# Twelve w_mod pieces moved from VectorE to TensorE strips in a two-block transformer kernel

## The chip, the cores and the metric

The kernel runs on one core of a Trainium2 chip. The metric is the time of one execution in microseconds on the device. The kernel before has a median of 2662.97 us over three runs, 2662.01 to 2665.58.

## The reference, cut to what matters

Two transformer blocks run over 256 tokens of width 2048, in float32. The change touches only the first block, and in it one of the six rows that a small vector `c` gives (`scale_m`):

```python
cond = jax.nn.silu(c)
mod = (cond @ w_mod[layer] + b_mod[layer]).astype(x.dtype)          # 2048 x 12288
shift_a, scale_a, gate_a, shift_m, scale_m, gate_m = [
    m[:, None, :] for m in jnp.split(mod, N_MOD, axis=-1)]
h = _rmsnorm(x, pre_mix_g[layer]) * (1.0 + scale_a) + shift_a
proj = h @ w_in[layer]
attn_out = _mla(...)                  # latent attention
rec_out = _hgrn2_bidir(...)           # gated recurrence, forwards and backwards
mix = jnp.concatenate([attn_out, rec_out], axis=-1) @ w_out[layer]
x = x + gate_a * _rmsnorm(mix, post_mix_g[layer])
h = _rmsnorm(x, pre_mlp_g[layer]) * (1.0 + scale_m) + shift_m
```

`w_mod` is 2048 x 12288, so one of the six rows needs 2048 x 2048 floats, 16 MB.

## The kernel before, in words

Every matrix product goes in chunks of 512 KB of weights. SyncE issues a chunk's DMA into one of 4 slots (`w_raw`), ScalarE rounds it (`w_hi`, L1267 or L1270), VectorE subtracts the rounded part (`w_lo`, `remainder`, L1742), and TensorE multiplies with both parts (L780 and L783 where the weights are stationary, L800 to L802 where the tokens are). A slot's DMA waits until VectorE has made `w_lo` of the chunk four before, ScalarE's rounding waits until TensorE has used that chunk (`chunk_used`), and TensorE waits for `w_lo`. So each engine may run up to four chunks ahead of the next one.

Each engine has one order of work, written out by hand. A list of phases (L363 on) says which chunks come; a function `beside` of each engine is called behind each chunk, and says what else that engine does there. The phases around the change are `in_f` (48 chunks), `in_hg` (16 chunks), `w_oa` (16), `w_or` (16), and then `up_0`.

The rows of `w_mod` come in **pieces** of 128 x 1024 floats (512 KB): piece (r, i) has rows 128 r to 128 r + 127 and half i of the columns, so a row of `mod` has 32 pieces. A list beside each phase gives each piece a chunk number. SyncE issues the piece's DMA behind that chunk's (`side`, L673) into one of 4 slots of `mod_w`, waiting until the piece four before is used up (`side_products`). VectorE multiplies it by its 128 values of silu(c) and adds it to `mod_acc` (`modulation`, L1812; the first two of a row write it with L1809) behind the same chunk. When all 32 are in, `sum_rows` adds up over the partitions: four matmuls with 32 columns of ones as weights, each into its own 32 partitions ("strips") of bank 4 of `ps` (L965). For `scale_m` that comes behind chunk 11 of `w_or`, and its pieces are spread so: 6 beside `in_hg` (chunks 1 to 6), 16 beside `w_oa` (chunks 4 to 15), 10 beside `w_or` (chunks 0 to 9).

Behind the chunks of `in_hg` and `w_oa` each engine also takes its part of the recurrence, `hgrn_step(g)`, with g counted through both phases. On TensorE: g = 2 the diagonal (L1105), g = 4 to 13 ten level steps of 128 small matmul records each (`level_step`, L1146), g = 15 and 17 wide levels (L1159), g = 19 `off_diagonal` (L1170), g = 21 `outputs` (L1178, L1179), g = 23 and 26 head sums (L1188, L1197). On VectorE level step s comes at g = s + 7: it waits for TensorE's (`level_mm`), selects (L2373) and updates queries, keys and forget gates (L2388, L2391, L2395); TensorE's step s needs the updates of step s - 2. The wide levels' updates are at g = 18 and 20. The level steps use banks 4 and 6 of `ps`; bank 5 is free from the time that VectorE has taken the row before out of it (`mods_done`), until `off_diagonal`.

Of the kernel before, what the change touches and what calls it, by code (L numbers as in the profile page):

```python
# [25 lines left out]
P = 128  # L26
T = 256
D = 2048
DT = D // P
# [4 lines left out]
NW = 512  # L34
SLOTS = 4
MW = 1024
# [91 lines left out]
FIRST_LO = {8: (6, 7), 4: (3, 3)}  # L128
FIRST_CHUNK = 8


# [26 lines left out]
def sides(pieces, chunks):  # L158

    return [(j, *piece) for j, piece in zip(chunks, pieces, strict=True)]  # L160
# [32 lines left out]
def build(nc, d, out):  # L193
    ctx = ExitStack()
    with ctx:
# [70 lines left out]
        a_diag = place("a_diag", [P, HEADS, 2, P], F32, x_at)  # L266
        a_units = a_diag[:].rearrange("p h s t -> p (h s) t")
        a_near = square.rearrange("p (u t) -> p u t", t=STRIP)
        hf = place("hf", [P, HEADS, T], F32, x_at + 8 * size_tile)
# [63 lines left out]
        def lin(*a, **k):  # L333
# [16 lines left out]
              for h in range(2)]  # L350
# [20 lines left out]
                  sides(gate_a[15:32] + shift_m, sorted([*range(4), *range(9, 48), 33, 35, 36, 40, 41, 43]))),  # L371
            Phase("in_hg", 1, [(l_g, i, 0) for i in range(4)], sides(scale_m[0:6], range(1, 7))),
            Phase("w_oa", 1, [(w_oa, i, 0) for i in range(4)], sides(scale_m[6:22], sorted([*range(4, 16), 5, 6, 8, 9]))),
            Phase("w_or", 1, [(w_or, i, 0) for i in range(4)], sides(scale_m[22:32], range(10))),
            Phase("up_0", 8, [(up[0], 0, 2), (up[0], 1, 2)], sides([(5, r, i) for r in range(2) for i in range(2)], (1, 3, 5, 7))),
# [28 lines left out]
        side_products = sem("side_products")  # L404
        mod_mm = sem("mod_mm")
        rows_summed, rows_kept = sem("rows_summed"), sem("rows_kept")
        gate_stored, row_2_landed = sem("gate_stored"), sem("row_2_landed")
# [347 lines left out]
        def _(pe):  # L755
# [149 lines left out]
            def beside(ph, j, first):  # L905
# [30 lines left out]
                if ph.name == "w_or" and j == 11:  # L936
                    pe.wait_ge(*o_1.row_moved(4))
                    pe.wait_ge(side_products, side_all("w_or"))
                    sum_rows(mod_acc)
                if ph.name == "down_0" and j == 1:  # L940
# [19 lines left out]

            def sum_rows(acc):

                sums = acc[:].rearrange("p g n -> p (g n)")
                for i in range(STRIPS):
                    mm = pe.matmul(ps[i * STRIP:(i + 1) * STRIP, 4, :], ones[:, 0:STRIP],  # L965
                                   sums[:, i * NW:(i + 1) * NW], start=True, stop=True)
                mm.then_inc(rows_summed, 1)
# [129 lines left out]
            def diagonal():  # L1097
# [9 lines left out]
                mm.then_inc(diag_mm, 1)  # L1107

            def hgrn_step(g):

# [7 lines left out]
                if 4 <= g < 4 + N_STEPS:  # L1118
                    level_step(g - 4)
                if g == 15:  # L1120
                    wide_level(NARROW)
# [41 lines left out]
            def off_diagonal():  # L1163
                pe.wait_ge(level_placed, 3)
                pe.wait_ge(level_updated, 6 * len(LEVELS))
                for way in range(2):
# [86 lines left out]
        def _(act):  # L1253
# [368 lines left out]
            def hgrn_step(g):  # L1622

                if g == 4:
                    act.wait_ge(diag_mm, 1)
                    act.copy(a_near, ps[:, 4, :].rearrange("p (u t) -> p u t", t=STRIP)).then_inc(diag_moved, 1)
                if g == 18:
                    act.wait_ge(level_selected, N_STEPS)
# [97 lines left out]
        def _(dve):  # L1726
# [24 lines left out]
            def beside(ph, it, j, first):  # L1751

                for piece in pieces_at(ph, j):
                    modulation(ph, it, first, *piece)
# [46 lines left out]
            def modulation(ph, it, first, n, section, r, i):  # L1801
# [5 lines left out]
                c = silu_c[:, bass.ds(it * 2 + (DT + r), 1)]  # L1807
                if first and r == 0:
                    ins = dve.tensor_scalar(acc, mod_w[:, slot, :], c, None, ALU.mult)  # L1809
# [755 lines left out]
```

## Time and profile before

| | |
|---|---|
| median of 3 runs | 2662.97 us |
| lowest, highest | 2662.01, 2665.58 us |
| the profiled execution | 2660.91 us |
| its span in the trace | 2659.0 us |
| TensorE busy | 2578.0 us (97%) |
| weight loads (PEld) busy | 2168.5 us (82%) |
| VectorE (DVE) busy | 1829.7 us (69%) |
| ScalarE (ACT) busy | 1216.9 us (46%) |
| DMA | 567.09 MB, mean 213 GB/s |

The profiled execution took 1.91 us more than its span, which lies around it, and is 2.06 us below the median. The phases in the trace: `in_hg` and its recurrence steps from about 385 us to 452 us, `w_oa` to 517 us, `w_or` to about 562 us, and the loop of `up_0` from about 590 us.

In the rows below, PE is TensorE's matmuls, PEld its weight loads, DVE VectorE, ACT ScalarE, SPq SyncE's queue. A float32 matmul stands in the trace as two records. "Idle before" in brackets is the time for which the engine had nothing under way, with what released it; "issue" means that the profile shows nothing that it waited for. The queue "instruction" carries the engines' programs.

### The profile page before, as it was taken

Reading aid. Unit: us, or ns where it says so; the run is one execution under the profiler, and the core shown is the slowest. Engines: PE = TensorE matmul, PEld = TensorE weight load, DVE = VectorE, ACT = ScalarE, POOL = GpSimd, SP = SyncE. Lnnn points to the kernel's source line nnn. Section 1 sums busy time; section 2 is a strip of 40 time slices with the busy share of each in tenths; the row PEclk is TensorE's granted clock in tenths of the full one; section 3 lists DMA queues with packets and bytes.
Section 4 is the critical chain, followed back from the end, with each engine's and each line's share of the span. In section 5 each row is a group of like instructions: output and inputs, shape, how many; then the busy total and the mean of one; then the engine's idle time right before and its main releaser. Section 6 shows DMA issues by size and latency. Waiting matters only on the chain.

```text
span 2659.0 us, 39728 instructions
## 1 busy us (share of the span) xinstructions
PE 2578.0 (97%) x15041; PEld 2168.5 (82%) x15041; DVE 1829.7 (69%) x2290; ACT 1216.9 (46%) x1562; POOL 58.4 (2%) x83
## 2 busy tenths in 40 slices
PE   6899999989999999999999999999999999999998
PEld 3588777868888888888888888878788888888887
DVE  5778899888864456645648888887666555555444
ACT  4354553464434344444544444465644444444343
POOL 2100000020000000000010000000000000000000
PEclk8999999999999999999999999999999999999999
DMA  9978794858866666565565655556466555566554
GB/s 359 362 256 306 233 344 161 299 185 293 282 206 226 195 188 186 188 197 184 175 212 179 199 175 167 167 180 201 150 198 189 189 187 186 187 189 207 194 193 158
DMA packets 413756, 567.09 MB, mean 213 GB/s; under 512 B 17997, under 2 KB 302066, under 8 KB 412736
## 3 DMA queue, kind: packets, MB, share of 16 engines
q1 hardware_dynamic: 408800, 548.72, 63.2%
q0 software_dynamic: 4832, 16.68, 1.8%
q8 instruction: 83, 1.36, 0.2%
q14 instruction: 41, 0.34, 0.0%
HBM read 563.22 MB, written 2.11 MB: 213 GB/s over the span
## 4 chain that ended last, share of the span: by engine, by line
PE 48%; DVE 2%; ACT 0%; issue 0%; DVEq 0%; ACTq 0%
PE ps L783 22%; PE ps L780 11%; PE ps L802 5%; PE ps L801 5%; PE ps L800 5%; DVE w_lo L1742 1%; PE ps L881 0%; PE ps L903 0%; DVE x_tok L2009 0%; DVE tmp L1849 0%; DVE pr L1829 0%; PE ps L837 0%; DVE ring L2159 0%; ACT pr L1708 0%; DVE pr L1856 0%
## 5 line engine op out<-in xcount | busy, mean ns | idle before, releaser
L1742 DVE TENSOR_TENSOR w_lo<-w_raw,w_hi 128x1024 fp32r<-128x1024 f32 (+1 forms) x870 | 1051.9, 1214 | 670.0 <-ACT w_hi L1267 347.6
L783 PE MATMUL ps<-acts,w_hi 128*128 128x512 f32 x4096 | 1321.7, 398 | 15.9 <-DVE w_lo L1742 7.8
L780 PEld LDWEIGHTS ps<-acts,w_lo 128*128 128x128 f32 x4096 | 769.9, 188 | 169.1 <-issue 1.2
L1270 ACT CAST w_hi<-w_raw 128x1024 fp32r<-128x1024 f32 (+1 forms) x542 | 563.7, 1044 | 647.5 <-PE ps L783 567.9
L780 PE MATMUL ps<-acts,w_lo 128*128 128x256 f32 x4096 | 828.4, 278 | 0.5 <-issue 0.5
L783 PEld LDWEIGHTS ps<-acts,w_hi 128*128 128x128 f32 x4096 | 640.2, 189 | 38.1 <-issue 15.2
L1267 ACT CAST w_hi<-w_raw 128x1024 fp32r<-128x1024 f32 x328 | 339.4, 1040 | 474.1 <-PE ps L802 393.5
L800 PE MATMUL ps<-w_hi,ff 128*128 128x512 f32 x864 | 336.3, 389 | 0.0
L802 PE MATMUL ps<-w_hi,ff 128*128 128x512 f32 x864 | 336.1, 389 | 0.0
L801 PE MATMUL ps<-w_lo,ff 128*128 128x512 f32 x864 | 336.1, 389 | 0.0
L800 PEld LDWEIGHTS ps<-w_hi,ff 128*128 128x128 f32 x864 | 162.2, 188 | 34.5 <-issue 0.8
L801 PEld LDWEIGHTS ps<-w_lo,ff 128*128 128x128 f32 x864 | 162.2, 188 | 33.9
L802 PEld LDWEIGHTS ps<-w_hi,ff 128*128 128x128 f32 x864 | 162.2, 188 | 33.3
L800 PE MATMUL ps<-w_hi,acts 128*128 128x512 f32 (+1 forms) x384 | 152.8, 398 | 4.4 <-DVE w_lo L1742 2.7
L1812 DVE SCALAR_TENSOR_TENSOR mod_acc<-mod_w,silu_c,mod_acc 128x1024 f32<-128x1024 f32 x120 | 151.9, 1277 | 0.0
L801 PE MATMUL ps<-w_lo,acts 128*128 128x512 f32 (+1 forms) x384 | 149.9, 390 | 0.0
L802 PE MATMUL ps<-w_hi,acts 128*128 128x512 f32 (+1 forms) x384 | 149.8, 390 | 0.0
L1829 DVE SCALAR_TENSOR_TENSOR pr<-pr,cols (+15 forms) x240 | 113.9, 475 | 10.9 <-DVE pr L1829 6.0
L1291 ACT COPY half_sum<-ps 128x512 f32<-128x512 f32 x154 | 89.6, 582 | 39.9 <-PE ps L783 39.9
L800 PEld LDWEIGHTS ps<-w_hi,acts 128*128 128x128 f32 x384 | 74.3, 193 | 29.9 <-issue 11.9
L802 PEld LDWEIGHTS ps<-w_hi,acts 128*128 128x128 f32 x384 | 74.2, 193 | 14.4
L801 PEld LDWEIGHTS ps<-w_lo,acts 128*128 128x128 f32 x384 | 74.4, 194 | 13.6
(331 smaller groups left out, 1542.1 us busy)
## 6 DMA issues: line engine op xcount, KB each, us to landing
w_raw<-in_w_in SPq DMA_DIRECT2D x216, 512.0 KB, 3.9
w_raw<-in_w_down SPq DMA_DIRECT2D x216, 512.0 KB, 4.5
w_raw<-in_w_gate_up SPq DMA_DIRECT2D x176, 512.0 KB, 3.6
mod_w<-in_w_mod SPq DMA_DIRECT2D x160, 512.0 KB, 6.3
w_raw<-in_w_up SPq DMA_DIRECT2D x128, 512.0 KB, 4.2
w_raw<-in_w_out SPq DMA_DIRECT2D x64, 512.0 KB, 4.7
mod_more<-in_w_mod SPq DMA_DIRECT2D x32, 512.0 KB, 12.0
w_raw<-in_w_in POOLq DMA_DIRECT2D x16, 512.0 KB, 7.2
```

The lines of the kernel that those rows point to most:

```text
L780: mm = pe.matmul(ps[:, bank, 0:T], w_lo[:, slot, k, c:c + P], lin_.act[:, kk, 0, :], start=False, stop=at_last and n == 0, skip_group_chec ...
L783: mm = pe.matmul(ps[:, bank, :], w_hi[:, slot, k, c:c + P], lin_.act[:, kk, :, :], start=at_first, stop=at_last and n == 1, skip_group_che ...
L800: pe.matmul(o, a_hi, hi, start=at_first, stop=False, skip_group_check=True)
L801: pe.matmul(o, a_hi, lo, start=False, stop=False, skip_group_check=True)
L802: mm = pe.matmul(o, a_lo, hi, start=False, stop=at_last, skip_group_check=True)
L1267: act.copy(wide[1][:, slot, 0:kn, 0:lin_.width], wide[0][:, slot, 0:kn, 0:lin_.width]).then_inc(hi_ready, 1)
L1270: act.copy(w_hi[:, slot, 0:kn, 0:lin_.width], w_raw[:, slot, 0:kn, 0:lin_.width]).then_inc(hi_ready, 1)
L1291: act.copy(half_sum[:, pair, 0:n, :], ps[:, 2 * pair:2 * pair + n, T:2 * T]).then_inc(half_ready, 1)
L1742: dve.tensor_tensor(low[cut], raw[cut], high[cut].bitcast(F32), ALU.subtract).then_inc(lo_ready, 1)
L1812: ins = dve.scalar_tensor_tensor(acc, mod_w[:, slot, :], c, acc, ALU.mult, ALU.add)
L1829: ins = dve.scalar_tensor_tensor(o, z_, w, o, ALU.mult, ALU.add)
```

## The change

- The 32 pieces of `scale_m` are dealt out anew. Twelve (rows r = 0 to 5, both halves) stand beside `in_hg`, two behind each of the chunks 1, 3, 9, 11, 13, 15. Thirteen stand beside `w_oa` (chunks 4 to 15, and 8 twice) and seven beside `w_or` (chunks 0 to 6).
- VectorE leaves out the twelve. TensorE multiplies them: at g = 3, 5, ..., 13 `strip_pieces(r)` does four matmuls with silu(c) of row r, spread to 32 columns, as weights and 512 columns of the piece moving, each into its strip of bank 5, and they add up there over r. It waits for both DMAs of the pair, and for r = 0 also for `mods_done`. VectorE's first pieces (L1809) are now those of r = 6.
- At g = 17 ScalarE copies bank 5 to `part_rows` (`part_moved`), having waited for all strips. `off_diagonal` waits for that copy. VectorE waits for the strips behind chunk 4 of `w_oa`, before its first piece.
- `sum_rows` behind chunk 11 of `w_or` does four more matmuls, which add `part_rows` in.

```diff
+STRIP_ROWS = 6
+        part_rows = ring[:, 2:4, :].rearrange("p k t -> p (k t)")
-            Phase("in_hg", 1, [(l_g, i, 0) for i in range(4)], sides(scale_m[0:6], range(1, 7))),
-            Phase("w_oa", 1, [(w_oa, i, 0) for i in range(4)], sides(scale_m[6:22], sorted([*range(4, 16), 5, 6, 8, 9]))),
-            Phase("w_or", 1, [(w_or, i, 0) for i in range(4)], sides(scale_m[22:32], range(10))),
+            Phase("in_hg", 1, [(l_g, i, 0) for i in range(4)], sides(scale_m[0:2 * STRIP_ROWS], sorted([1, 3, *range(9, 5 + 2 * STRIP_ROWS, 2)] * 2))),
+            Phase("w_oa", 1, [(w_oa, i, 0) for i in range(4)], sides(scale_m[2 * STRIP_ROWS:25], sorted([*range(4, 16), 8]))),
+            Phase("w_or", 1, [(w_or, i, 0) for i in range(4)], sides(scale_m[25:32], range(7))),
...
                 if ph.name == "w_or" and j == 11:
                     pe.wait_ge(*o_1.row_moved(4))
                     pe.wait_ge(side_products, side_all("w_or"))
-                    sum_rows(mod_acc)
+                    pe.wait_ge(part_moved, 1)
+                    sum_rows(mod_acc, True)
...
+            def sum_rows(acc, part=False):
                 sums = acc[:].rearrange("p g n -> p (g n)")
+                if part:
+                    for i in range(STRIPS):
+                        row = C_IDENT + i * STRIP
+                        pe.matmul(ps[i * STRIP:(i + 1) * STRIP, 4, :], consts[:, row:row + 1].to_broadcast([P, STRIP]),
+                                  part_rows, start=True, stop=False, skip_group_check=True)
...
+            def strip_pieces(r):
+                ph = by_name["in_hg"]
+                if r == 0:
+                    pe.wait_ge(mods_done, 8)
+                for i in range(D // MW):
+                    n = ph.piece0 + 2 * r + i
+                    pe.wait_ge(mod_landed[n % MOD_SLOTS], 16 * (len(PIECE_OF) // 4 + n // MOD_SLOTS + 1))
+                for strip in range(STRIPS):
+                    slot, c = (ph.piece0 + 2 * r + strip // 2) % MOD_SLOTS, strip % 2 * NW
+                    mm = pe.matmul(ps[strip * STRIP:(strip + 1) * STRIP, 5, :],
+                                   silu_c[:, DT + r:DT + r + 1].to_broadcast([P, STRIP]), mod_w[:, slot, c:c + NW],
+                                   start=r == 0, stop=r == STRIP_ROWS - 1, skip_group_check=True)
+                mm.then_inc(side_products, 2)
...
                 if 4 <= g < 4 + N_STEPS:
                     level_step(g - 4)
+                if 3 <= g < 3 + 2 * STRIP_ROWS and g % 2:
+                    strip_pieces((g - 3) // 2)
...
             def off_diagonal():
                 pe.wait_ge(level_placed, 3)
+                pe.wait_ge(part_moved, 1)
...
+                if g == 17:
+                    act.wait_ge(side_products, side_all("in_hg"))
+                    act.copy(part_rows, ps[:, 5, :]).then_inc(part_moved, 1)
...
-                for piece in pieces_at(ph, j):
+                if ph.name == "w_oa" and j == 4:
+                    dve.wait_ge(side_products, side_all("in_hg"))
+                for piece in pieces_at(ph, j) if ph.name != "in_hg" else ():
                     modulation(ph, it, first, *piece)
...
-                if first and r == 0:
+                if first and r == (STRIP_ROWS if section == 4 else 0):
```

## Rows read from the trace of the kernel before

**Rows 1.** Busy time by stretch: start:end, length, then us (records) per engine.
```profile
390.00:450.00 60.00, 53.90 (x1622) 45.70 (x1621) 58.09 (x63) 17.48 (x20) 0.00 (x0) 1.00 0.46 141
450.00:500.00 50.00, 48.85 (x453) 41.42 (x452) 44.98 (x42) 29.73 (x38) 0.00 (x0) 1.00 0.82 295
500.00:560.00 60.00, 56.26 (x257) 44.79 (x256) 51.38 (x50) 29.97 (x44) 0.00 (x0) 0.97 0.75 264
600.00:770.00 170.00, 170.00 (x970) 148.03 (x969) 144.50 (x155) 71.49 (x76) 0.00 (x0) 1.00 0.85 281
```
**Rows 2.** Timeline of PE, 390 to 450 us: seven of eight rows with idle time.
```profile
397.93 0.73 PE L783 MATMUL ps<-acts,w_hi 128*128 128x512 f32 x2 [1.02 <-issue]
...
401.47 0.27 PE L1146 MATMUL ps<-hq,kf 128*32 128x16 f32 x10 [0.54 <-issue]
...
406.57 0.40 PE L1146 MATMUL ps<-qb,kb 128*32 128x16 f32 x26 [0.84 <-issue]
...
423.55 1.27 PE L1146 MATMUL ps<-qb,kb 128*32 128x16 f32 x128 [0.78 <-DVE hb L2395]
...
432.97 1.27 PE L1146 MATMUL ps<-qb,kb 128*32 128x16 f32 x128 [0.71 <-DVE hb L2395]
...
435.86 0.39 PE L780 MATMUL ps<-acts,w_lo 128*128 128x256 f32 x2 [0.49 <-issue]
...
440.41 0.30 PE L1146 MATMUL ps<-hq,kf 128*32 128x16 f32 x11 [1.42 <-issue]
```
**Rows 3.** Timeline of PE: first wide level, then four of five rows with idle time.
```profile
450.63 0.22 PE L1159 MATMUL ps<-hq,kf 128*32 128x32 f32 x1
...
466.42 2.02 PE L1170 MATMUL ps<-hq,kf 128*128 128x128 f32 x16 [1.15 <-DVE hb L2395]
...
509.99 0.50 PE L800 MATMUL ps<-w_hi,att_out 128*128 128x512 f32 x1 [0.64 <-DVE w_lo L1742]
...
517.02 0.47 PE L800 MATMUL ps<-w_hi,acts 128*128 128x512 f32 x1 [0.52 <-DVE w_lo L1742]
...
544.78 0.47 PE L800 MATMUL ps<-w_hi,acts 128*128 128x512 f32 x1 [2.15 <-DVE w_lo L1742]
```
**Rows 4.** Timeline of PE around `sum_rows` of `scale_m`.
```profile
557.16 0.39 PE L802 MATMUL ps<-w_hi,acts 128*128 128x512 f32 x1
557.48 1.06 PE L965 MATMUL ps<-mod_acc,ones 128*32 128x512 f32 x8
558.47 0.50 PE L800 MATMUL ps<-w_hi,acts 128*128 128x512 f32 x1
```
**Rows 5.** Timeline of DVE: a piece of `in_hg`, the first level step, the first wide update.
```profile
400.99 1.28 DVE L1812 SCALAR_TENSOR_TENSOR mod_acc<-mod_w,silu_c,mod_acc 128x1024 f32<-128x1024 f32 x1
402.19 1.22 DVE L1742 TENSOR_TENSOR w_lo<-w_raw,w_hi 128x1024 fp32r<-128x1024 f32 x1
403.32 0.73 DVE L2373 COPY_PREDICATED ring<-masks,ps 128x256 f32<-128x256 uint8 x1
...
452.09 1.22 DVE L2388 TENSOR_TENSOR hq<-hq,hf 128x1024 f32<-128x1024 f32 x1
```
**Rows 6.** Timeline of SyncE's queue: chunks 10 and 11, then 12 of `in_hg`.
```profile
401.10 2.70 SPq L663 DMA_DIRECT2D w_raw<-in_w_in  x2
409.25 0.37 SPq L663 DMA_DIRECT2D w_raw<-in_w_in  x1
```
**Rows 7.** Timelines of DVE and ACT ahead of the idle time at 544.78 us.
```profile
536.88 1.28 DVE L1812 SCALAR_TENSOR_TENSOR mod_acc<-mod_w,silu_c,mod_acc 128x1024 f32<-128x1024 f32 x1
538.08 1.21 DVE L1888 TENSOR_TENSOR y<-y,ps 128x1024 f32<-128x1024 f32 x1
...
539.39 0.64 ACT L1333 ACTIVATE ring<-y 128x512 f32<-128x512 f32 x1 [3.68 <-DVE y L1888]
```
**Rows 8.** Busy time by stretch, around the same idle time; the column behind POOL is the granted clock.
```profile
546.00:549.00 3.00, 3.00 (x8) 2.30 (x7) 3.00 (x3) 0.22 (x1) 0.00 (x0) 0.50 0.69 227
```
**Rows 9.** DMA queues, 400 to 450 us: the instruction queue.
```profile
q8 instruction: 11, 0.18, 1.4%
```

More of the change, by code:

```diff
@@ L405, in build @@
         mod_mm = sem("mod_mm")
+        part_moved = sem("part_moved")
         rows_summed, rows_kept = sem("rows_summed"), sem("rows_kept")
@@ L959, in turn_vectors @@
                                  consts[0:rows, C_IDENT:C_IDENT + rows]).then_inc(cols_turned, 1)
-            def sum_rows(acc):
+            def sum_rows(acc, part=False):
                 sums = acc[:].rearrange("p g n -> p (g n)")
+                if part:
[3 more added lines that the diff above has]
+                                  part_rows, start=True, stop=False, skip_group_check=True)
                 for i in range(STRIPS):
                     mm = pe.matmul(ps[i * STRIP:(i + 1) * STRIP, 4, :], ones[:, 0:STRIP],
-                                   sums[:, i * NW:(i + 1) * NW], start=True, stop=True)
+                                   sums[:, i * NW:(i + 1) * NW], start=not part, stop=True, skip_group_check=True)
                 mm.then_inc(rows_summed, 1)
```

## Prediction

> **What bounds the kernel now.** I read the page first: TensorE is busy for 97% of the span, so a change pays only if TensorE has less work or waits less. Then the busy time by stretch, over the phases that the change touches [rows 1]. From 390 to 560 us TensorE stands idle for 6.10 + 1.15 + 3.74 = 11.0 of 170 us, and behind that, from 600 to 770 us, for nothing. So 11 us is all that shorter waits can give here, and every microsecond of new TensorE work comes off it. The reader is to see a second thing in the first stretch: VectorE is busy for 58.1 of 60 us. It looks like the bound, and VectorE is what the change relieves. Only then the timeline of TensorE, for who ends each wait. Of the 6.10 us up to 450 us, VectorE's updates end three waits, 0.78 + 0.17 + 0.71 = 1.66 us [rows 2] (two of them have rows); 4.31 us carry "issue", in five places. (The rest are shreds at the stretch's edges.) From 450 us on it is VectorE each time [rows 3]: 1.15 us in front of `off_diagonal`, three waits of 0.64 + 0.43 + 0.52 = 1.59 us at the turn from `w_oa` to `w_or` (the first and the last have rows), and 2.15 us in `w_or`. VectorE is full in the recurrence, but TensorE is hardly less so: this is a balance, not a bound on one side.
>
> **The change part by part.**
>
> *Strips, six groups of four matmuls.* The nearest row is `sum_rows`, which has the same shape: 32 columns of weights, 512 moving, four strips. Eight records take 1.06 us together, and the next chunk's first matmul starts 558.47 - 557.16 = 1.31 us after the last one, where the plain pitch is 0.23 us [rows 4]. So a group costs 1.08 us, and six cost 6.5 us. All lie in TensorE's own order between chunks 3 and 14 of `in_hg`; only idle time can hide them.
>
> *Which idle time.* The piece at 400.99 us and the one before it at 398.66 us leave VectorE; each takes 1.2 us from start to start [rows 5], and the four before them lie ahead of a wait for TensorE's diagonal and bring nothing. So VectorE could be 2.4 us earlier at its first level step (403.32 us). But that step waits for TensorE's, which starts at 399.75 us and has a gap of 0.54 us in it (it ends near 401.7 us), and is now one group later: about 402.8 us. VectorE gains 0.5 us at once, and from there TensorE falls behind by 1.08 us every second step, so its waits for VectorE end: 1.66 us back. Net up to the wide levels: 6.5 - 1.66 = +4.8 us. From the wide level at g = 15 VectorE's updates start when TensorE's matmuls end, now as before (450.63 us plus 1.2 us [rows 3] against VectorE's 452.09 us [rows 5]), so the 1.15 us in front of `off_diagonal` stays, and TensorE is still 4.8 us late behind it.
>
> *Fewer pieces in `w_oa`.* Chunks 5, 6 and 9 lose one each. The one behind chunk 9 stands ahead of the head sums on VectorE and of chunks 10 to 15. SyncE also gets past chunk 12's piece earlier, which today holds up the load of x and chunk 13 until 487.5 us. I make VectorE 1.2 us (its own piece) to 2.0 us (with chunk 13's transfer in time) earlier by 500 us. The three waits of the turn ask for 0.64, 0.43 and 0.52 us, one behind the other, 1.59 us in all. I take all of it: -1.6 us; the bound is none of it.
>
> *Fewer pieces in `w_or`.* The wait at 544.78 us has a chain that can be read: the piece behind chunk 7 at 536.88 us, then the sum at 538.08 us, then ScalarE's squares at 539.39 us, behind which stands the rounding of chunk 8 [rows 7]. That piece is gone, so the chain is 1.2 us shorter and the wait 0.95 us. After the 2.15 us wait the granted clock fell to 0.50, that is 1.2 GHz, from 546 to 549 us [rows 8]; after the waits of 1.42 and 1.15 us it stayed at 1.00. With matmuls of half speed those 3 us do the work of 1.5 us. I count 1.2 + 1.6 = -2.8 us (the 1.6 being the excess of start-to-start times from 545.54 to 549.64 us). Bounds: 0 and -3.8 us.
>
> *`sum_rows`.* Eight more records in one run with the others: +1.0 us by the same row [rows 4]; nothing hides it, TensorE is full there.
>
> *New waits.* TensorE's wait for the pieces: pair r = 0 and 1 are issued by about 379 us, 16 us ahead of use. Pair 2 follows chunk 9 near 399 us, for use at 417 us. Pair 3 stands behind chunk 11, which goes out at about 403 us [rows 6], and its slot comes free only with the strips of g = 5, near 409 us. So here **SyncE does wait for a slot**, for some 6 us, against what the change says of itself. Behind it is chunk 12, which isn't due before 409.25 us [rows 6] and is used near 437 us. Pairs 4 and 5 wait likewise, 4 us each, in front of chunks with equal slack. Price: 0. ScalarE's wait and copy at g = 17 delay its rounding of the next chunk, which then waits for TensorE anyhow: 0. `off_diagonal`'s new wait and VectorE's at chunk 4 of `w_oa` are for things done 15 us before: 0.
>
> *Transfers beside level steps.* The five "issue" gaps sum to 4.31 us, all in or right behind runs of 128 small matmuls, and a packet of the instruction queue (11 of them, 16 KB each, in 50 us [rows 9]) lies 1 to 3 us before each. I read them as TensorE waiting for its program. Eight more pieces now run between 399 and 434 us beside those packets, while each strip group gives 1 us of work for 16 records, which lets packets catch up. The trace has no price for either; bounds are -2.75 us (the gaps at 406, 435 and 440 us hidden) and, four pairs times the longest gap, 4 x 1.42 = +5.7 us. I take 0.
>
> The Trainium skill ("Runtime: NRT & Kernel Launch", Instruction fetch mechanics) has the program fetched in 16 KiB blocks, which the packets' size bears out, and calls the cost of crossing a block "mostly hidden". By that page this term is 0 and the gaps need another cause; the rows show 4.31 us that isn't hidden.
>
> **Sum.** +6.5 - 1.66 - 1.6 - 2.8 + 1.0 = +1.4 us. On the profiled execution, 2660.91 us, that gives 2662.3 us; it lies 2.06 us below the median, so against the median: **2664.4 us**. Of the 15.3 us of VectorE work taken away (twelve at 1.28 us), next to nothing arrives, because TensorE pays 7.5 us for it.
>
> **The rivals.**
> - *TensorE's gaps take the strips in.* The three gaps above vanish and the wait in `w_or` goes fully: 2664.4 - 2.75 - 0.95 = 2660.7 us. For: the groups stand where blocks run short. Against: the transfers move into the same microseconds.
> - *VectorE was the bound after all.* The strips cost nothing, everything is 2.4 us earlier at `off_diagonal`: -2.4 - 1.6 - 2.8 + 1.0 = -5.8 us, 2657.2 us. For: 58.1 of 60 us busy. Against: TensorE's 1.66 us of waits for it.
> - *Transfers starve TensorE's program* (slower). Each of the four pairs between 399 and 434 us holds a block back by up to 1.42 us: 2664.4 + 5.7 = 2670.1 us. It decides once a block lands later than TensorE has run through the one before, in 3 to 4 us.
> - *The late waits stay.* VectorE's and ScalarE's chains in `w_oa` and `w_or` hang on TensorE's own late results (`outputs`, head sums), so they shift by the 4.8 us too and the gains of 4.4 us don't come: 2668.8 us. Against: pieces leave these chains wherever they stand.
>
> **How the numbers follow.** A measurement of this kernel tells about 0.2%, 5.3 us, from no change: the borders are 2657.6 and 2668.3 us. Chances: the forecast (2661 to 2667 us) 0.56, gaps take the strips 0.15, VectorE the bound 0.05, program starved 0.12, late waits stay 0.12. Of the last two I count some part within the border. Faster 0.05, same 0.77, slower 0.18. The range of 2659.5 to 2669.5 us takes in all but the second rival and the third's far half.
>
> **What would show it.** After the change: L1146's waits for VectorE up to 450 us gone; TensorE's first wide-level matmul 4 to 6 us later than 450.63 us (earlier than 450 us says that VectorE was the bound); new strip records of about 1.06 us a group; "issue" gaps near 4.3 us in sum (over 8 us: starved); the three waits of the turn gone; the wait in `w_or` near 1 us with the clock at 1.00 behind it. I am wrong above all if the gaps move much either way, or if the waits in `w_oa` and `w_or` don't shrink.

## The result and the profile after

The changed kernel takes 2666.7 us (median of 14 runs, 2664.0 to 2671.29), the kernel before, run in turn with it, 2661.61 us (14 runs, 2658.31 to 2666.02). The ratio is 1.0016, with a 95% interval of 1.0009 to 1.0024: 2.4 to 6.4 us slower. Compared a second time (e7 below) it was 1.0009 (0.9999 to 1.0018), so the size of the loss is known to some 2 us only. Every ratio below is to executions of the kernel before that ran in turn with it. Two single executions, 5430.18 us in e2 and 5185.93 us in e7, took twice as long as all others and stand in no ratio.

| | before | after |
|---|---|---|
| profiled execution, span | 2659.0 us | 2664.7 us |
| TensorE busy | 2578.0 us | 2591.4 us |
| VectorE busy | 1829.7 us | 1816.8 us |
| diagonal (first record) to first wide level | 391.47 to 450.63 us: 59.16 | 391.68 to 462.18 us: 70.50 |
| wide level to the spread of the gate row (`w_or`, chunk 3) | to 527.98 us: 77.35 | to 536.99 us: 74.81 |
| from there to the end of the span | 2131.0 us | 2127.7 us |

So all the loss stands in the level steps, +11.3 us, and 2.5 + 3.3 us come back behind them. Of the 3.3 us, 2.9 us come back ahead of `up_0`'s first matmul (579.14 us before, 585.26 us after, so 51.2 and 48.3 us behind the spread). From there to the end the code is the same, and the fourteen traces of this document need 2078.3 to 2081.6 us for it: a difference of 1 or 2 us in whole spans tells nothing of the change. Here is the busy time by stretch of the changed kernel, in the columns of [rows 1]:

```profile
390.00:450.00 60.00, 52.81 (x1491) 40.52 (x1490) 47.75 (x49) 14.43 (x16) 0.00 (x0) 0.94 0.53 175
450.00:500.00 50.00, 48.36 (x588) 40.70 (x584) 39.81 (x42) 29.08 (x37) 0.00 (x0) 1.00 0.69 238
500.00:560.00 60.00, 59.70 (x281) 49.45 (x278) 51.85 (x50) 30.76 (x45) 0.00 (x0) 1.00 0.74 266
```

From 500 to 560 us TensorE idles 0.3 us, where it was 3.7 us. From 390 to 450 us VectorE is busy for 47.8 us instead of 58.1 us, and TensorE idles more than before, 7.2 us, at a mean granted clock of 0.94. Its timeline has every wait (the rows that answer to [rows 2] and [rows 3]):

```profile
401.46 0.36 PE L1172 MATMUL ps<-hq,kf 128*32 128x16 f32 x18 [0.37 <-issue]
...
408.20 0.66 PE L1172 MATMUL ps<-qb,kb 128*32 128x16 f32 x33 [2.48 <-issue]
...
419.21 0.82 PE L1172 MATMUL ps<-qb,kb 128*32 128x16 f32 x75 [0.40 <-issue]
...
432.87 0.50 PE L786 MATMUL ps<-acts,w_hi 128*128 128x512 f32 x1 [0.55 <-issue]
...
438.79 0.40 PE L1172 MATMUL ps<-hq,kf 128*32 128x16 f32 x12 [2.47 <-issue]
...
477.33 2.02 PE L1197 MATMUL ps<-hq,kf 128*128 128x128 f32 x16 [0.51 <-DVE hb L2427]
...
526.02 0.47 PE L803 MATMUL ps<-w_hi,acts 128*128 128x512 f32 x1 [0.30 <-DVE w_lo L1772]
```

Two more gaps, 0.93 us near 429 us and 1.13 us near 454 us, make the sum of "issue" 8.33 us. VectorE ends no wait before 477 us: the engine that the change relieved is not the one that TensorE waits for here. Behind the two long gaps the clock is halved. Busy time by stretch again, with the clock in the column behind POOL:

```profile
408.20:411.00 2.80, 2.79 (x43) 1.13 (x44) 2.04 (x3) 0.00 (x0) 0.00 (x0) 0.50 0.13 45
...
438.80:442.00 3.20, 3.20 (x21) 2.78 (x22) 2.73 (x4) 0.00 (x0) 0.00 (x0) 0.50 0.05 15
```

0.50 is 1.2 GHz, in each case after an idle time of TensorE of 2.47 or 2.48 us; at half clock these two stretches did the work of 3.0 us in 6.0 us.

What stood ahead of the gap at 408 us? SyncE's queue, with the start and length of each run of issues:

```profile
398.99 0.37 SPq L666 DMA_DIRECT2D w_raw<-in_w_in  x1
399.40 1.53 SPq L676 DMA_DIRECT2D mod_w<-in_w_mod  x2
400.98 0.98 SPq L666 DMA_DIRECT2D w_raw<-in_w_in  x2
410.68 0.82 SPq L676 DMA_DIRECT2D mod_w<-in_w_mod  x2
411.55 3.12 SPq L666 DMA_DIRECT2D w_raw<-in_w_in  x2
```

Five transfers of 512 KB leave within 3 us. From 401.5 to 405.5 us the queues then show nothing but that data, and only from 405.5 us the packet with TensorE's program:

```profile
q1 hardware_dynamic: 564, 1.28, 96.7%
...
q8 instruction: 1, 0.02, 11.9%
```

(The first row is of 401.5 to 405.5 us, the second of 405.5 to 406 us: packets, MB, share of 16 engines.) TensorE goes on 2.7 us behind that, at 408.20 us. At 410.68 us the wait for a slot that the prediction named has ended: two pieces and chunk 12 leave in one go.

### The profile page after: what moved, and what is told of

It is laid out like the page before. It is cut to its first block, busy times and chain, and to the rows that moved or that the text cites. A ratio compares the mean times of both kernels' runs of the same rounds, so it can differ in the third digit from the quotient of the medians.

```text
span 2664.7 us, 39824 instructions
## 1 busy us (share of the span) xinstructions
PE 2591.4 (97%) x15097; PEld 2175.8 (82%) x15097; DVE 1816.8 (68%) x2278; ACT 1217.7 (46%) x1563; POOL 58.4 (2%) x83
## 4 chain that ended last, share of the span: by engine, by line
PE 74%; DVE 3%; ACT 1%; issue 0%; POOL 0%; DVEq 0%; ACTq 0%; POOLq 0%
PE ps L786 31%; PE ps L783 15%; PE ps L803 9%; PE ps L805 9%; PE ps L804 9%; DVE w_lo L1772 1%; DVE x_tok L2041 0%; PE ps L884 0%; PE ps L906 0%; DVE tmp L1881 0%; POOL ring L731 0%; DVE pr L1861 0%; DVE pr L1888 0%; PE ps L840 0%; DVE ring L2191 0%
## 5 line engine op out<-in xcount | busy, mean ns | idle before, releaser
L1844 DVE SCALAR_TENSOR_TENSOR mod_acc<-mod_w,silu_c,mod_acc 128x1024 f32<-128x1024 f32 x108 | 137.0, 1280 | 0.0
## 6 DMA issues: line engine op xcount, KB each, us to landing
mod_more<-in_w_mod SPq DMA_DIRECT2D x32, 512.0 KB, 11.6
```

What stands on the lines that cost most here:

```text
L1844: ins = dve.scalar_tensor_tensor(acc, mod_w[:, slot, :], c, acc, ALU.mult, ALU.add)
```

## The experiments

To read them it helps to time the packet by hand. I looked through the instruction queue in steps of half a microsecond and noted, for the gap in the second level step, when the gap before it ended (a block had just come in), when the next packet showed, and when TensorE went on:

| | gap before ended | packet | went on | idle |
|---|---|---|---|---|
| before | 401.47 | 404.0 | 406.57 | 0.84 |
| after | 401.46 | 405.5 | 408.20 | 2.48 |
| after, again | 400.52 | 405.0 | 407.54 | 2.75 |
| small transfers | 402.85 | 405.0 | 407.67 | 0.55 |
| spread | 399.13 | 401.5 | 403.95 | 0.55 |
| four on VectorE | 402.19 | 405.5 | 407.83 | 1.39 |

From packet to matmul it is 2.3 to 2.7 us in this table (the packets are read on a grid of 0.5 us). What differs is how long the packet takes to show: 4.0 and 4.5 us where five transfers left together, 2.2 to 3.3 us elsewhere.

A packet is a **block** of the program, 16 KB. The gaps of the changed kernel stand 256 TensorE instructions apart, or a multiple of that (matmul records, weight loads and its sequencer's instructions counted together, one off at most): they are the borders of the blocks.

**Theory A:** the new transfers hold back TensorE's program. **Theory B:** it counts where the borders of the program's blocks fall among the small matmuls. A third question is what the strips cost by themselves.

### e1_small_transfers

```diff
+                wide_ = 8 if ph.name == "in_hg" and r >= 2 else MW
-                sp.dma_start(mod_w[:, slot, :], w_mod[bass.ds(it * (2 * P) + r * P, P), col:col + MW]
+                sp.dma_start(mod_w[:, slot, 0:wide_], w_mod[bass.ds(it * (2 * P) + r * P, P), col:col + wide_]
```

> The changed kernel, but the eight pieces r = 2 to 5 move only 8 of their 1024 columns (4 KB instead of 512 KB), so that scale_m comes out of partly stale data; waits, strips and records are the same. Theory A (the new transfers hold back TensorE's program): a packet of the instruction queue starts 0.7 to 1.6 us after the block before it is used up, not 3 to 4 us; the gap of 2.48 us at 408 us falls to 0 to 0.8 us and that of 2.47 us at 439 us to 0.5 to 1.4 us, the clock stays at 1.00 there, the issue gaps up to 456 us sum to 3 to 5 us instead of 8.3 us, the first wide level starts at 456 to 458 us instead of 462.2 us, and the time is 4 to 6 us below the changed kernel's. Theory B (only where the block borders fall among the small matmuls counts): the same gaps, the wide level at 462 us, no change in time.

Measured: ratio to the kernel before 0.9987 (0.9977 to 0.9996), so 0.29% or 7.7 us below the changed kernel's 1.0016, and the intervals don't touch. Diagonal to wide level: 64.6 us. Gaps: 5.65 us in sum instead of 8.33 us. The two long ones became

```profile
407.67 0.46 PE L1173 MATMUL ps<-qb,kb 128*32 128x16 f32 x33 [0.55 <-issue]
...
435.05 0.31 PE L1173 MATMUL ps<-hq,kf 128*32 128x16 f32 x12 [1.36 <-issue]
```

and the clock is 1.00 from 391 to 470 us. The gaps stand at the same records of the same steps (33 and 12 records before the end), so the borders are where they were; only their length changed. Theory A holds, B alone doesn't. The ratio also lies clear of the changed kernel's second interval (0.9999 to 1.0018). With the transfers small, the change would have been a gain.

### e2_narrow_strips

```diff
+                    wide_ = NW if r == 0 else 16
-                    mm = pe.matmul(ps[strip * STRIP:(strip + 1) * STRIP, 5, :], ... mod_w[:, slot, c:c + NW],
+                    mm = pe.matmul(ps[strip * STRIP:(strip + 1) * STRIP, 5, 0:wide_], ... mod_w[:, slot, c:c + wide_],
```

> The changed kernel, but the strips of r = 1 to 5 have 16 columns instead of 512 (rest of those rows of scale_m left out); transfers, waits and the number of records are the same. A group then costs about 0.15 us instead of 1.08 us. Theory A: the strips' own work, 5 x 0.9 = 4.6 us, goes, but a block is used up earlier, so 1 to 2 us come back as longer gaps and waits for VectorE; wide level at 458 to 459 us. Theory that strips are the main loss and transfers harmless: wide level at 457.5 us or earlier and gaps in sum not above 8.3 us. Theory that VectorE bounds the steps: no change at the wide level.

Measured: ratio 0.9997 (0.9987 to 1.0008), 5 us below 1.0016, though these intervals just meet (1.0008, 1.0009). Diagonal to wide level: 67.2 us instead of 70.5 us (wide level at 460.2 us, somewhat later than I expected), with gaps of 9.5 us in sum, one of 2.50 us and one of 2.74 us. So the long gaps need no strips, and 1.2 us of the 4.6 us of strip work taken away stood again as gaps.

### e3_after_pad

```diff
                 turn_vectors([0])
+                for _ in range(25):
+                    pe.matmul(ps[0:STRIP, 7, 128:136], ident[:, 0:STRIP], consts[:, C_IDENT:C_IDENT + 8], ...)
```

> The changed kernel with 25 tiny float32 matmuls (100 records) in TensorE's order at the start of the program, where TensorE waits for its first data. Work is the same; only the borders of program blocks lie 50 matmul records earlier in the level steps: at record 60 instead of 110 of the first. Theory B (borders count): the wrap out of a step into a chunk comes two steps earlier, and a second wrap comes before the wide level; gaps move to record 60 in step 0, 44 in step 1, and the pair of gaps now at 433 and 439 us comes near 423 us and again near 450 us; 1 to 3 us slower or, if a border misses the bursts of transfers, as much faster. Theory A alone: the gap by the first burst (near 406 us) stays 2 to 2.5 us long, only its place in the step shifts; time within 1 us.

Measured: ratio 1.0012 (1.0003 to 1.0022), the changed kernel's time. The gaps did move as the count of records says: that of the second step now has 82 of 128 records behind it (46 ahead; 44 were expected).

```profile
406.34 1.30 PE L1175 MATMUL ps<-qb,kb 128*32 128x16 f32 x82 [2.60 <-issue]
...
445.96 0.85 PE L1175 MATMUL ps<-qb,kb 128*32 128x16 f32 x78 [2.85 <-issue]
```

The one trace has 75.0 us from diagonal to wide level and 11.1 us of gaps, 4.5 us worse than the changed kernel's, but the runs of 3 rounds don't show such a loss. The gaps lie at the borders of blocks; which borders they are is not worth a measurable time. And a single trace of this stretch can be several microseconds off the mean, a warning for my own reading of the kernel before.

### e6_before_again and e7_after_again

No edit.

> The kernel before, once more, to see how much the gaps that carry 'issue' vary between executions of one program. The trace of before has 59.1 us from the diagonal to the first wide level, and the same code in the w_or experiment 62.8 us. If the gaps are chance (a packet meets a transfer or not), this one lies between 58 and 64 us; if they are fixed by the program, at 59.1 us within 0.3 us. Time ratio 1.000.

> The changed kernel, once more. From the diagonal to the first wide level 67 to 73 us (70.5 us in its first trace), with at least one gap over 2 us and half clock behind it; time 1.0005 to 1.0025 of the kernel before.

Measured: ratios 0.9994 (0.9984 to 1.0004) and 1.0009 (0.9999 to 1.0018). The kernel before this time took 63.1 us from diagonal to wide level, with 8.42 us of issue gaps where [rows 2] has 4.31 us, and no wait for VectorE at all:

```profile
421.59 0.82 PE L1146 MATMUL ps<-hq,kf 128*32 128x16 f32 x74 [0.59 <-issue]
426.41 0.95 PE L1146 MATMUL ps<-qb,kb 128*32 128x16 f32 x90 [0.56 <-issue]
431.51 1.09 PE L1146 MATMUL ps<-hq,kf 128*32 128x16 f32 x106 [0.85 <-issue]
436.61 1.22 PE L1146 MATMUL ps<-qb,kb 128*32 128x16 f32 x122 [0.84 <-issue]
441.55 0.58 PE L780 MATMUL ps<-acts,w_lo 128*128 128x256 f32 x2 [2.59 <-issue]
```

These are the very steps that stood behind VectorE in the first trace. The gaps take the place of those waits when packets come later: a border 16 records further in each step (74, 90, 106, 122). The changed kernel took 68.9 us, with gaps of 2.75 and 2.45 us. Behind the first of them the clock stayed at 1.00:

```profile
407.54 0.46 PE L1172 MATMUL ps<-qb,kb 128*32 128x16 f32 x33 [2.75 <-issue]
...
407.54:411.00 3.46, 3.46 (x54) 2.39 (x55) 2.92 (x3) 0.00 (x0) 0.00 (x0) 1.00 0.42 96
```

Four traces then: 59.2 and 63.1 us (e4, the same code up to here, has 62.8 us) against 70.5 and 68.9 us, a loss of 5.8 to 11.3 us.

### e8_before_transfers

```diff
+                    if ph.name == "in_hg" and j in (10, 11, 13, 15):
+                        ...
+                        for i in range(2):
+                            slot = (2 * extra_loads[0] + i) % MOD_SLOTS
+                            sp.dma_start(mod_w[:, slot, :], w_mod[i * P:(i + 1) * P, 0:MW]).then_inc(extra_landed, 16)
```

> The kernel before with eight more transfers of 512 KB that nobody uses, two behind each of chunks 10, 11, 13 and 15 of in_hg, into free mod_w slots; no strips, nothing else changed, the result is the same. Theory A: TensorE's issue gaps between the diagonal and the first wide level grow from 4.3 us to 7 to 9 us though no engine has more work; the way from diagonal to wide level takes 62 to 66 us, in part taken from waits for VectorE; 1 to 4 us slower than before. Rival (strips, not transfers, make the gaps): 59 to 63 us, as before, and no change in time.

Measured: gaps of 9.9 us in sum and 66.4 us from diagonal to wide level, both somewhat above what I expected, against 59.2, 62.8 and 63.1 us (gaps of 4.3, 7.5 and 8.4 us) in the three traces of that code without the transfers. New among them:

```profile
417.83 0.68 PE L1159 MATMUL ps<-qb,kb 128*32 128x16 f32 x58 [1.95 <-issue]
...
435.43 1.55 PE L1159 MATMUL ps<-hq,kf 128*32 128x16 f32 x106 [2.45 <-issue]
```

No engine has more work there. The ratio is 1.0003 (0.9993 to 1.0012), 0.0009 above e6 with intervals that overlap: the trace says what theory A expects, the time leaves it open.

### e5_spread and e10_spread_again

```diff
-sides(scale_m[0:2 * STRIP_ROWS], sorted([1, 3, *range(9, 5 + 2 * STRIP_ROWS, 2)] * 2))
+sides(scale_m[0:2 * STRIP_ROWS], (1, 1, 3, 3, 11, 12, 13, 14, 15, 15, 15, 15))
```

> The changed kernel with the same twelve pieces in strips, but their transfers one behind each of chunks 11, 12, 13, 14 and four behind 15 (instead of two behind 9, 11, 13, 15), so that no five transfers go out together and SyncE hardly waits for a slot. Theory A (a packet of TensorE's program waits behind the transfers that are queued at that moment): the 2.48 us gap near 408 us falls to about 1 us and that near 439 us stays 1.4 to 2.5 us; the way from the diagonal to the first wide level takes 65 to 68 us instead of 70.5 us; 2 to 4 us below the changed kernel, so level with the kernel before (within 0.1%). Rival (the volume in this stretch counts, not its bunching): 70 us and the time of the changed kernel.

> The spread version once more, beside the one with four pieces on VectorE, on the same chip: 64 to 67 us from diagonal to wide level; ratio to the kernel before 0.9990 to 1.0005.

Measured: 64.9 and 65.2 us from diagonal to wide level, ratios 0.9996 (0.9987 to 1.0005) and 1.0001 (0.9992 to 1.0010). The same twelve pieces, the same bytes in the same stretch, 3.6 to 5.7 us shorter in the traces, about as much as e1 won by leaving the bytes out. e5's interval doesn't touch the changed kernel's first one (1.0009 to 1.0024), e10's just does, and both overlap its second. So how the transfers are placed counts. One long gap stayed, behind chunk 11 of `in_hg`, in both traces (3.84 and 3.56 us):

```profile
422.47 1.16 PE L1172 MATMUL ps<-qb,kb 128*32 128x16 f32 x116 [0.41 <-issue]
429.31 0.80 PE L786 MATMUL ps<-acts,w_hi 128*128 128x512 f32 x1 [3.84 <-issue]
```

SyncE's queue of this kernel says why: the four pieces behind chunk 15 were again a burst of five transfers with that chunk.

```profile
420.94 0.37 SPq L666 DMA_DIRECT2D w_raw<-in_w_in  x1
421.35 4.09 SPq L676 DMA_DIRECT2D mod_w<-in_w_mod  x4
425.93 0.38 SPq L666 DMA_DIRECT2D w_raw<-in_w_out  x1
```

A packet had shown at 420.0 us, the next only at 426.5 us, and TensorE went on at 429.31 us. That suggests sending every piece alone.

### e12_one_each

```diff
 ...
                     for piece in pieces_at(ph, j):
-                        side(ph, 0, *piece)
+                        if ph.name != "in_hg" or piece[0] < 9:
+                            side(ph, 0, *piece)
+                    if ph.name == "w_oa" and j < 3:
+                        side(by_name["in_hg"], 0, 9 + j, *by_name["in_hg"].side[9 + j][1:])
```

> The changed kernel, all twelve pieces in strips at its own level steps, with its transfers never more than one behind a chunk from chunk 11 on: one behind each of the diagonal chunks 11 to 15, and the last three one behind each of the first three chunks of the next weight. Theory (bunches): the gap of 3.84 and 3.56 us that both spread kernels kept behind level step 11 falls to 2 us or less, the stretch from the diagonal products to the first wide level takes 61.5 to 63.5 us (64.9 and 65.2 in those, 70.5 in the changed kernel), ratio 0.999 to 1.000. Rival (volume or block borders): a gap of about 3.5 us stays and the stretch takes about 65 us, ratio 1.000.

Measured: ratio 1.0000 (0.9991 to 1.0009), 67.7 us from diagonal to wide level (392.4 to 460.1 us), gaps of 7.23 us in sum (e5: 4.98 us). The burst is gone from the queue, and the gap behind chunk 11 is half as long. But two more stand behind it, where e5 had none:

```profile
430.68 0.50 PE L789 MATMUL ps<-acts,w_hi 128*128 128x512 f32 x1 [1.91 <-issue]
...
436.32 0.30 PE L1175 MATMUL ps<-hq,kf 128*32 128x16 f32 x12 [2.18 <-issue]
...
448.62 0.64 PE L1175 MATMUL ps<-hq,kf 128*32 128x16 f32 x53 [1.57 <-issue]
```

The one gap came out as theory A said, the stretch did not: even the rival's 65 us was too little. So a burst is not the whole cause. The times at which packets showed tell more:

| | packets show at (us) | data meanwhile |
|---|---|---|
| before | 408.0, 412.0, 416.0, 420.0, 424.5, 429.0, 433.0, 437.5 | 108 to 123 GB/s |
| before, again | 409.5, 413.5, 419.0, 424.0, 429.0, 434.0, 439.0 | 108 GB/s |
| one each | 408.0, 412.5, 418.0, 423.0, 428.0, 433.5, 438.0, 446.0 | 210 to 213 GB/s |
| spread | 409.5, 415.0, 420.0, 426.5, 430.5, 434.5, 439.5 | 205, 291, then 93 GB/s |

(GB/s from the busy time in the stretches of 10 us from 410 to 440 us.) In the first trace of before a packet comes every 4.0 to 4.5 us, about as fast as TensorE runs through them; in the second mostly every 5.0 us, and that is its row of short gaps. With a chunk and a piece every 5 us it is 4.5 to 5.5 us and once 8 us, and three of the blocks in the table have TensorE idle ahead of them or in them for 0.84, 1.91 and 2.18 us. Across a burst it is 6.5 us, and behind that 4.0 to 5.0 us. But these distances hold TensorE's own time for a block too, so they don't measure a delay: the changed kernel has 7.3 us between two packets (439.90 and 447.22 us) beside only 54 GB/s.

The delay shows from the border on. In each trace one packet shows behind each border, and no matmul behind the next border starts less than 2.2 us after that packet: it is the next block that it brings. A transfer is under way from its issue until it has landed. Counted over the 159 borders between 395 and 452 us in the fourteen traces: where all transfers under way land within 2 us of the border (60 borders), the packet shows 1.1 us behind it (median; 2.5 us at most); where the last one lands more than 5 us later (19 borders), 3.6 us (median; 2.3 to 4.7 us).

A block of the level steps without strips or waits takes TensorE 4.05 us, and 2.2 to 2.8 us pass from packet to matmul, so a gap opens once the packet shows later than about 1.8 us. All ten packets that showed later than 4 us had transfers under way that landed 4.8 us or more behind the border. One of them is e12's, with no burst: the border at 441.94 us lies 1 us behind the issue of a chunk and a piece, the packet shows 4.4 us later, and TensorE goes on at 448.62 us. That points to what is under way at the moment when TensorE crosses a border, rather than to bursts as such. A burst makes a bad moment likely, single pieces still have some, and so has the kernel before, whose packets showed 2.5 to 2.8 us behind the borders from 417 to 437 us in e6 and 0.2 to 2.0 us in the first trace. This is read from the traces alone; no run moved a single transfer against a border.

e12 has 2.9 us more than e5 in this stretch, of which 2.25 us are gaps. Why the time in all is the same stays open; the trace of one execution doesn't resolve it.

### e4_before_w_or

```diff
-            Phase("w_or", 1, [(w_or, i, 0) for i in range(4)], sides(scale_m[22:32], range(10))),
+            Phase("w_or", 1, [(w_or, i, 0) for i in range(4)], sides(scale_m[22:32], (*range(7), 8, 9, 10))),
```

> The kernel before with one edit: the pieces of w_or stand behind chunks 0 to 6, 8, 9 and 10 instead of 0 to 9, so that none stands between chunk 7 and the sum of the first panel on VectorE. No strips. My reading of the wait at 544.78 us: it falls from 2.15 us to about 1 us and the clock stays at 1.00, so the first spread behind it is met and the time is 2 to 3 us (0.1%) below the kernel before. Rival (transfers, not VectorE's piece, end that wait): the wait stays 2 us, the clock drops, no change in time.

Measured: ratio 0.9996 (0.9987 to 1.0005). The wait did shrink as the chain said, from 2.15 to 0.83 us (1.92 us in e6), but another came behind it:

```profile
548.20 0.47 PE L800 MATMUL ps<-w_hi,acts 128*128 128x512 f32 x1 [0.83 <-DVE w_lo L1742]
...
561.65 0.47 PE L800 MATMUL ps<-w_hi,acts 128*128 128x512 f32 x1 [1.32 <-DVE w_lo L1742]
```

By their order the three late pieces now stand ahead of the next panel's sum; that they make the second wait was not tested. The reading of the chain was right, the price of 2 to 3 us wasn't shown: nothing measurable was left of it.

### e9_four_on_vector

```diff
+DVE_ROWS = 2
...
-sides(scale_m[0:2 * STRIP_ROWS], sorted([1, 3, *range(9, 5 + 2 * STRIP_ROWS, 2)] * 2))
+sides(scale_m[0:2 * STRIP_ROWS], (*range(1, 9), 12, 13, 14, 15))
...
-                if 3 <= g < 3 + 2 * STRIP_ROWS and g % 2:
-                    strip_pieces((g - 3) // 2)
+                if 5 <= g < 5 + 2 * (STRIP_ROWS - DVE_ROWS) and g % 2:
+                    strip_pieces((g - 5) // 2 + DVE_ROWS)
...
-                for piece in pieces_at(ph, j) if ph.name != "in_hg" else ():
+                for piece in pieces_at(ph, j) if ph.name != "in_hg" or j <= 2 * DVE_ROWS else ():
```

> The changed kernel, but the first four pieces (rows 0 and 1) stay on VectorE behind chunks 1 to 4 of in_hg, where it waits for TensorE's diagonal anyhow, and only rows 2 to 5 go through four strip groups at g = 5, 7, 9, 11; transfers one behind each of chunks 1 to 8 and 12 to 15. By my reading two groups at 1.08 us go (-2.2 us), and no two pieces leave together: diagonal to first wide level 61 to 64 us (e5 64.9, changed kernel 68.9 and 70.5), the gains in w_oa and w_or stay (wide level to the gate row's spread 74.8 us instead of 77.4 to 78.1), so 3 to 6 us below the changed kernel and 1 to 3 us (0.05 to 0.1%) below the kernel before. Rival (VectorE's four pieces come back on its path in front of the level steps): 66 us and the time of the kernel before or above.

Measured: ratio 0.9998 (0.9989 to 1.0007), 64.8 us from diagonal to wide level. Its median, 2661.12 us, is 2.4 us below that of the second spread version (2663.54 us), less than either spreads over its own runs, and it is no better than the kernel before. Gaps: 6.33 us. Two strip groups fewer did not show in the stretch (64.8 against 64.9 and 65.2 us): the gap in the second step was 1.39 us, as in e6, where e5 had 0.55 us, and one in the seventh step 2.15 us.

### e11_four_one_each

```diff
-sides(scale_m[0:2 * STRIP_ROWS], (*range(1, 9), 12, 13, 14, 15))
+sides(scale_m[0:2 * STRIP_ROWS], (*range(1, 5), 11, 12, 13, 14, 15, 15, 15, 15))
-                if 5 <= g < 5 + 2 * (STRIP_ROWS - DVE_ROWS) and g % 2:
-                    strip_pieces((g - 5) // 2 + DVE_ROWS)
+                if 7 <= g < 7 + 2 * (STRIP_ROWS - DVE_ROWS) and g % 2:
+                    strip_pieces((g - 7) // 2 + DVE_ROWS)
```

Against e9, and with the same move of the last three pieces behind the first chunks of `w_oa` as in e12.

> Scale rows 0 and 1 stay on VectorE as in the kernel before, rows 2 to 5 go through strips at level steps 7, 9, 11 and 13 only, and no two pieces of the scale weight are issued together: pieces 4 to 8 stand one behind each of the diagonal chunks 11 to 15, and pieces 9 to 11 one behind each of the first three chunks of the next weight. Theory (several transfers issued together hold up TensorE's instructions): no gap on TensorE between the diagonal products and the first wide level is longer than about 1.5 us, the stretch takes 61 to 63.5 us (59.1 before, 64.8 in the four-strip kernel with its pieces in bunches), and the ratio to the kernel before is 0.998 to 0.9995. Rival (the bytes in the stretch or the borders of instruction blocks hold them up, not the bunches): gaps of 2.5 us and more stay, the stretch takes 64 to 66 us, ratio 0.9995 to 1.001.

Measured: ratio 0.9996 (0.9987 to 1.0005), 66.0 us from diagonal to wide level (393.46 to 459.42 us), gaps of 7.70 us, the longest

```profile
437.22 0.40 PE L790 MATMUL ps<-acts,w_hi 128*128 128x512 f32 x1 [3.24 <-issue]
```

with no burst anywhere near: SyncE sent a chunk and one piece at 430.0 us, 2 us ahead of the border at 431.85 us, and again at 434.4 us; the packet showed 3.1 us behind that border. The rival has the stretch (64 to 66 us) and the theory doesn't; after this run and e12 the idea that single pieces are free doesn't hold. No version that does the whole work beat the kernel before beyond its interval, and the five with spread transfers or four strips (e5, e9 to e12) are all within 0.04% of it.

## Why the prediction was right, and where it wasn't

The forecast was 2664.4 us, +1.4 us, in a range of 2659.5 to 2669.5 us, with no change beyond 0.2% as the likeliest case. Measured were 2666.7 us and 1.0016. The sign and the reason were right: TensorE pays for the strips and VectorE's time is worth little. By the ratio the loss is 4.3 us, so the size was 2.9 us short (1.0 us by the second comparison). But it is in part luck that the time fell into the range: the stretch itself went wrong. The wide level came 11.55 us later than 450.63 us, where 4 to 6 us were forecast, and the gaps, 8.33 us, passed the 8 us that I had named as the sign of a starved program. What hid this in the total is that more came back behind the stretch than forecast. By its terms:

- **Strips, +6.5 us.** Confirmed in size: the changed kernel's groups take 1.06 us each, as at 419.89 and 430.36 us in its trace, but the one at half clock (408.66 us) took 2.0 us. e2 gives 5 us for five groups by time, 3.3 us in the trace. Without the transfers' bytes, though, gaps take a part of them in, as the first rival had it: e1 has all six groups and only 1.5 us more in the stretch than e6 (64.6 and 63.1 us), with gaps of 5.65 us against 8.42 us and no fall of the clock, where e6 has one behind 2.59 us.
- **Waits for VectorE end, -1.66 us.** They are gone from the trace. But they were a property of one trace: in e6 the kernel before has none, and gaps in their place. This term is better counted as 0, and that is one part of the shortfall.
- **Transfers beside level steps, 0, with bounds of -2.75 and +5.7 us.** This is the step that failed. I had both bounds, saw packets 1 to 3 us ahead of each gap, and chose the middle for want of a price. Against a single trace of before the gaps grew from 4.31 to 8.33 us. The better measure is e1: without the transfers' bytes the kernel is 7.7 us faster (5.9 us against the second comparison), 4.3 to 5.9 us shorter in this stretch. So the rival "transfers starve TensorE's program" happened, and what it cost was in part given back further down. How the transfers are placed takes a part of that loss away (e5, e10: 64.9 and 65.2 us), but none of the placements gives the ratio of e1, 0.9987, where the bytes are gone (though e1's interval, up to 0.9996, overlaps theirs).
- **The clock, not in the sum.** I priced a fall of the clock in `w_or` and forgot it where I made gaps longer. Two gaps of 2.5 us cost about 2.8 us more: the 256 instructions behind the first took 6.35 us, and 4.87 us in e7, where the clock stayed at 1.00; those behind the second took 5.56 us, and 4.3 us in e1 (a gap left out). It doesn't follow idle time alone: behind 2.75 us at 407.54 us of e7 and 1.92 us in `w_or` of e6 it stayed at 1.00, behind 2.15 us in the kernel before it fell [rows 8]. With it the stretch adds up: 6.5 + 4.0 (gaps) - 1.7 (waits for VectorE) + 2.8 = 11.6 us, and 11.3 us were measured between the two traces.
- **`w_oa`, -1.6 us.** More came: -2.5 us (77.35 to 74.81 us), and -3.3 us between e6 and e7 (78.1 to 74.8 us), with 74.8 or 74.9 us in eight traces of the new split (changed kernel, e1, e2, e3, e5, e7, e10, e12) and 75.3 us in e9 and e11. Beside the three waits of the turn (one of 0.30 us stays), the wait in front of `off_diagonal` fell from 1.15 to 0.51 us; I had kept it whole. The rest I can't place.
- **`w_or` and `sum_rows`, -2.8 + 1.0 us.** Up to `up_0`'s first matmul, -2.9 us against the first trace of before and -1.7 us between e6 and e7 (49.9 to 48.3 us). The wait is gone whole, where I left 0.95 us. The 1.6 us for the clock was in the one trace and not in the other.
- **The slot that SyncE waits for, 0.** It does wait, from 402 to 410.68 us, 8.7 us where I gave 6 us. Harmless for chunk 12 itself, as predicted. But it does what I didn't see: it gathers two pieces and the next chunk, so that they leave together, and TensorE's packets wait behind that. I priced the wait for those who need the data, not for those who share the queues with it.
- Of the Trainium skill I had cited ("Runtime: NRT & Kernel Launch", Instruction fetch mechanics) that crossing a block is mostly hidden. In the level steps it isn't: 128 records with their weight loads are run through in 1.3 us, a packet needs 2.2 to 2.8 us from showing to use, and came up to 7 us behind the one before it (398.5 to 405.5 us of the changed kernel).

Not settled: by which path a packet waits behind data (which of the 16 engines, in which order) no run here shows; whether a transfer moved away from a border takes the gap with it, as the count over the borders suggests; and what sets the borders and the transfers differently against each other from one execution to the next (4.31 and 8.42 us of gaps in the kernel before). e8, which put eight transfers alone into the kernel before, cost 0.0009 against e6 with intervals that overlap, so the price of the transfers rests on e1 and on e5 against the changed kernel, both in the presence of the strips.

## What to carry over

Small matmuls make TensorE run through its program fast, and there its program is one more stream that waits while data is moved: don't put several big transfers into such a stretch at once, and if the kernel can take them elsewhere, put none (one at a time, the stretch still took 66.0 and 67.7 us here); and look for "issue" gaps before calling an idle DMA queue free. An engine that is 97% busy in a stretch need not be the bound; count the other engine's waits for it, in more than one trace, before buying it relief with the other's time. A wait in SyncE's queue that delays nothing can still bunch what stands behind it.

## What the runs showed of the hardware

From the showing of a 16 KB program packet to the next matmul it took 2.2 to 2.8 us in all 85 'issue' gaps of more than 0.3 us between 395 and 470 us in the fourteen traces, whatever else ran. Behind each border of TensorE's program (every 256 of its instructions) one packet showed: 1.1 us behind it (median) where the transfers under way landed within 2 us, 3.6 us (median, 4.7 us at most) where they landed more than 5 us later. The same code can have issue gaps of 4.31 or of 8.42 us in this stretch from one execution to the next.

TensorE's clock was at 0.50 behind idle times of 1.95 us (e8), 2.03 us (e4), 2.15, 2.18, 2.47, 2.48, 2.59, 3.24 and 3.84 us, and once behind 1.62 us (at 585.26 us of the changed kernel), and at 1.00 behind one of 1.92 us (e6) and one of 2.75 us (e7).
